# GpSimd asks for the down blocks of the first mixture, on a queue and semaphores of their own

## The reference, cut to what matters

```python
D_FF_EXPERT = 7 * D_MODEL // 2      # 3584
N_EXPERTS, TOP_K = 8, 2

def swiglu(xn, w_gu, w_down):
    g, u = jnp.split(xn @ w_gu, 2, axis=-1)
    return (jax.nn.silu(g) * u) @ w_down

def moe_swiglu(xn, router, w_gu, w_down):
    logits = (xn @ router).astype(jnp.float32)
    top_v, top_i = lax.top_k(logits, TOP_K)
    w = jax.nn.softmax(top_v, axis=-1)
    comb = jnp.sum(jax.nn.one_hot(top_i, N_EXPERTS, dtype=jnp.float32) * w[..., None],
                   axis=-2).astype(xn.dtype)
    out = jnp.zeros_like(xn)
    for e in range(N_EXPERTS):
        out = out + comb[..., e:e + 1] * swiglu(xn, w_gu[e], w_down[e])
    return out
```

## Time and profile before

| | us |
|---|---|
| median of the runs | 2438.81 (2438.15 to 2439.09, 3 runs) |
| the profiled execution | 2440.72, its span 2438.9 |
| first mixture, TensorE's first gate/up product to its last scatter | 799.9 to 1672.8 |
| HBM read over the span | 641.66 MB |
| issues of od_moe_gu into the ring and z | 196 + 28, of 1024 KB |
| issues of od_moe_down into the ring and z | 49 + 7, of 2048 KB |

### The profile page before, as it was taken

One profiled execution on the slowest core, in us unless ns is written; L12 is line 12 of the kernel. 1 busy time (PEld: TensorE's weight loads), 2 busy tenths in 40 slices (PEclk: granted clock), 3 DMA queues, 4 the chain that ended last, 5 costly groups with the idle time before them and its releaser, 6 DMA issues.

```text
span 2438.9 us, 34641 instructions
## 1 busy us (share of the span) xinstructions
PE 2341.8 (96%) x14916; PEld 1345.8 (55%) x14916; DVE 687.9 (28%) x1507; ACT 376.7 (15%) x813; POOL 1.2 (0%) x9
## 2 busy tenths in 40 slices
PE   8899999999999999999998999998989999989997
PEld 6777888888577333333333333335766336746433
DVE  2565121139765101011010101011232122273122
ACT  2101100010111111110110111111132111163211
POOL 0000000000000000000000000000000000000000
PEclk9899999999999999999999999998999999999998
DMA  9489245374366798999999999996622995832690
GB/s 319 164 296 359 72 166 214 132 265 141 115 223 250 295 380 339 374 385 408 405 409 405 408 405 409 395 395 254 235 69 75 338 317 157 214 114 75 213 357 36
DMA packets 281384, 645.13 MB, mean 265 GB/s; under 512 B 14699, under 2 KB 99969, under 8 KB 281217
## 3 DMA queue, kind: packets, MB, share of 16 engines
q1 hardware_dynamic: 278444, 637.64, 71.2%
q10 hardware_dynamic: 2773, 5.11, 0.6%
HBM read 641.66 MB, written 1.05 MB: 264 GB/s over the span
## 4 chain that ended last, share of the span: by engine, by line
PE 88%; DVE 6%; SPq 2%; ACT 2%; issue 1%; DMA 1%; ACTq 0%; DVEq 0%
PE bank L1613 20%; PE bank L1299 20%; PE bank L1715 11%; PE bank L1650 7%; PE bank L1538 6%; PE bank L1550 3%; PE bank L1319 3%; DVE att L3372 2%; PE bank L1642 2%; SPq L1205 2%; PE bank L1775 2%; PE bank L1734 1%; PE bank L1701 1%; PE bank L1861 1%; PE bank L1348 1%
## 5 line engine op out<-in xcount | busy, mean ns | idle before, releaser
L1613 PE MATMUL bank<-ring,xn 128*32 128x512 f32 (+1 forms) x3520 | 465.9, 594 | 2.3 <-DMA ring<-od_moe_gu 2.3
L1299 PE MATMUL bank<-xn,ring 128*128 128x256 f32 x2048 | 452.0, 383 | 3.3 <-ACT xn L2286 1.1
L1299 PEld LDWEIGHTS bank<-xn,ring 128*128 128x128 f32 x2048 | 392.0, 192 | 60.3 <-issue 8.1
L1613 PEld LDWEIGHTS bank<-ring,xn 128*32 128x32 f32 (+1 forms) x3520 | 140.2, 115 | 304.2 <-issue 301.5
L1715 PE MATMUL bank<-ring,att 128*32 128x512 f32 x2208 | 247.9, 593 | 1.3 <-ACT att L2416 1.3
L2979 DVE TENSOR_TENSOR sq<-att,bank 32x512 f32<-32x512 f32 x70 | 48.0, 686 | 414.4 <-ACT att L2427 412.9
L1715 PEld LDWEIGHTS bank<-ring,att 128*32 128x32 f32 x2208 | 72.3, 110 | 160.1 <-issue 159.7
L1538 PE MATMUL bank<-xn,ring 128*128 128x256 f32 x704 | 152.8, 379 | 0.0
L1538 PEld LDWEIGHTS bank<-xn,ring 128*128 128x128 f32 x704 | 134.1, 191 | 17.9
L2427 ACT ACTIVATE att<-bank 64x512 f32<-64x512 f32 (+1 forms) x123 | 72.4, 589 | 376.1 <-PE bank L1613 291.6
L2416 ACT COPY att<-bank 128x384 f32<-128x384 f32 (+1 forms) x72 | 29.9, 450 | 520.3 <-PE bank L1701 400.1
(11 more groups left out here) (352 smaller groups left out, 1968.7 us busy)
## 6 DMA issues: line engine op xcount, KB each, us to landing
ring<-od_moe_gu SPq DMA_DIRECT2D x196, 1024.0 KB, 15.5
ring<-od_moe_down SPq DMA_DIRECT2D x49, 2048.0 KB, 17.3
ring<-ada_w SPq DMA_DIRECT2D x24, 2048.0 KB, 8.2
ring<-moe_w_gate SPq DMA_DIRECT2D x32, 1024.0 KB, 11.6
ring<-moe_w_up SPq DMA_DIRECT2D x32, 1024.0 KB, 9.7
ring<-moe_w_down SPq DMA_DIRECT2D x16, 2048.0 KB, 13.8
z<-od_moe_gu SPq DMA_DIRECT2D x28, 1024.0 KB, 13.8
ring<-ev_w_in SPq DMA_DIRECT2D x10, 2048.0 KB, 20.4
```

The source lines that it names most:

```text
L1299: mm = nc.tensor.matmul(ps[:, c * T:(c + 1) * T], kblk(b)[:, k, u * T + c * P:u * T + (c + 1) * P], x[:, k, :], start=k == 0, stop=k == KD ...
L1613: mm = nc.tensor.matmul(PSB[r.fill.b][j * w:(j + 1) * w, :], xn[:, k, at:at + w], rows_[:, half, c * WBLK:(c + 1) * WBLK], start=k == 0, s ...
```

## The change

The blocks that `down_block` makes are kept in a list, `downs`. Eight new semaphores, `down_landed`, one for each slot, count the down blocks that land; `slot_landed` counts all other blocks. Each block's count (`b.landed`) is made anew from the list before the engines' programs are written. SyncE's two loops over the blocks of the first mixture leave the down blocks out. GpSimd, when its constants are set, walks through the down blocks of the same experts in the same order: it waits for the release of the earlier block of the slot, asks for the load, and adds to `down_landed`. Before the second expert it waits for `order_ready` and reads each expert's number into a register of its own, as SyncE does. TensorE's `landed` waits for the one or the other semaphore. Loads, slots, their order in the ring and all computation are as they were.

```diff
--- before.py
+++ after.py
@@ -357,6 +357,7 @@
         zero_row = no_bits.unsqueeze(1).to_broadcast([P, 4, P])
 
 
+        down_landed = [sem(f"down_landed{i}") for i in range(SLOTS + 1)]
         slot_landed = [sem(f"slot_landed{i}") for i in range(SLOTS + 1)]
         bank_full = [sem(f"bank_full{b}") for b in range(8)]
         bank_free = [sem(f"bank_free{b}") for b in range(8)]
@@ -661,8 +662,11 @@
             r.tile = [(tile_full[j], count(tile_full[j], 1) + 1) for j in range(tiles - 1)] + [(bank_full[f.b], f.n)]
             return r
 
+        downs = []
+
         def down_block(st, x, load, tiles):
             x.down = block(*load(x.c, WBLK))
+            downs.append(x.down)
             x.used = [(hid_used, st.used + x.c + 1)] + [(tile_down[j], count(tile_down[j], 1) + 1) for j in range(tiles - 1)]
             x.down.other_tiles = x.used
 
@@ -1182,6 +1186,12 @@
         rows_landed = sem("rows_landed")
 
 
+        in_slot, down_in_slot = [0] * (SLOTS + 1), [0] * (SLOTS + 1)
+        for b in blocks:
+            n = down_in_slot if b in downs else in_slot
+            n[b.slot] += len(b.loads)
+            b.landed = 16 * n[b.slot]
+
         block_ = ctx.enter_context(nc.Block())
 
         @block_.sync
@@ -1215,14 +1225,16 @@
                 free_slot(i)
                 load(i)
             for i in range(*moe1[0].blocks):
-                free_slot(i)
-                load(i, 0)
+                if blocks[i] not in downs:
+                    free_slot(i)
+                    load(i, 0)
             sp.wait_ge(order_ready, 1)
             for st in moe1[1:]:
                 expert = sp.value_load(order[0:1, st.rank:st.rank + 1], min_val=0, max_val=E1 - 1)
                 for i in range(*st.blocks):
-                    free_slot(i)
-                    load(i, expert)
+                    if blocks[i] not in downs:
+                        free_slot(i)
+                        load(i, expert)
 
             sp.wait_ge(excess_ready, 1)
             with sp.If(sp.value_load(order[0:1, E1:E1 + 1], min_val=0, max_val=T) > CAPS[0]):
@@ -1278,6 +1290,21 @@
             nc.gpsimd.tensor_copy(early_mask, con("causal")).then_inc(masks_set, 1)
             nc.gpsimd.tensor_copy(ident_bits, ident).then_inc(masks_set, 1)
 
+            def load_downs(st, expert):
+                for b in blocks[slice(*st.blocks)]:
+                    if b in downs:
+                        if b.earlier.release is not None:
+                            pool.wait_ge(*b.earlier.release)
+                        for tile in b.earlier.other_tiles:
+                            pool.wait_ge(*tile)
+                        dst, src = b.loads[0](b)(expert)
+                        pool.dma_start(dst, src).then_inc(down_landed[b.slot], 16)
+
+            load_downs(moe1[0], 0)
+            pool.wait_ge(order_ready, 1)
+            for st in moe1[1:]:
+                load_downs(st, pool.value_load(order[0:1, st.rank:st.rank + 1], min_val=0, max_val=E1 - 1))
+
         @block_.tensor
         def _(pe):
             def open_bank(f):
@@ -1287,7 +1314,7 @@
                 return PSB[f.b]
 
             def landed(b):
-                pe.wait_ge(slot_landed[b.slot], b.landed)
+                pe.wait_ge((down_landed if b in downs else slot_landed)[b.slot], b.landed)
 
             def unit(b, u, f, x, ready=None):
```

## The result

| | us |
|---|---|
| after, median of the runs | 2478.64 (2477.38 to 2480.02, 4 runs) |
| before, beside it | 2438.95 (2438.15 to 2443.07, 4 runs) |
| ratio | 1.0159, 95% interval 1.0142 to 1.0177 |
| the profiled execution after | 2477.38, its span 2475.7 |

The change makes the kernel slower by 39.7 us, and by the interval by 35 to 43. The forecast was +16, with a range up to +29: right in sign and in the place of the waits, too small by more than half.

A forecast was written before the change was run, and what follows sets the result against it. Prediction: TensorE bounds wide experts, loads the paired ones. Gains and costs of requests 0; downs passing gate/up blocks cost 10.1 + 5.8 = 15.9, say +16 us: 2454.8 us, 8 in 10 range 2436 to 2468.

The forecast's parts named there:

- What bounds the kernel: First mixture: TensorE bounds wide experts, loads bound paired ones once the ring's lead is gone; loading order can win 9.2 us.
- Part 1: SyncE no longer waits at down blocks' slots and saves 56 issues: nothing is unblocked, gain 0.
- Part 2: GpSimd makes 56 waits and requests, low end 0.37 us each; harmless under 10 us a piece: cost 0.
- Rival (c): GpSimd's requests over 10 us each or held up, downs themselves late: 2465 to 2480 us, chance 0.06.
- Part 3, no bandwidth to win: Two queues sharing the DMA engines move no more than one: 405 GB/s against 406 and 407.
- rival (b): Two requesters fill the DMA engines better, so the kernel gets faster, 2430 us at 7% more rate; chance 0.13.
- Part 3, passing downs, G17 in each paired expert: Downs on the second queue delay each paired expert's last gate/up block: +10.1 us for the first two together, +5.8 third.
- so I take equal shares while both have work: Both load queues get half the rate; last gate/up block 5.8 us late in first and third paired experts.
- one third for 2 KB rows: Upper case: queues alternate by rows, so paired experts' last two gate/up blocks get a third: +12.4 + 11 = +23.
- the transfers never pause from 1077 to 1340: Loads run unbroken through the first two paired experts, so the later date holds alone: +10.1 us, 5.8 not added.
- one common date: First two paired experts: delay set by the second's last gate/up landing, 1332.7 against 1320.4: +10.1 us together.
- The signs: Profile after: 117 MB third queue, downs landing under 12 us, gate/ups over 18, waits only at paired experts' last gate/up block.

The follow-up runs named there:

- e8: Kernel before, with the first mixture's experts reordered so that two wide ones stand between every two paired ones: 2427.69 us, ratio 0.9950.
- e11: Changed kernel with 44 products of zeros on TensorE ahead of the wait for each paired expert's last gate/up block: 2472.59 us, ratio 1.0124.

## Why the prediction was wrong

- **What bounds the kernel: held.** Of the 9.2 us of waits nothing else could be won, and e8 won them by the lead alone.
- **Part 1, SyncE's waits, 0: held.** 179 of its 224 gate/up requests now last under 0.5 us, and no time came of it.
- **Part 2, GpSimd's requests, 0: held.** 0.74 us each, twice the low end that I took, and far under the 10 us from which it would have mattered. Rival (c) is out. VectorE's port did no harm that these rows show.
- **Part 3, no bandwidth to win: held.** 401 and 402 GB/s with two queues, against 406 and 407; rival (b) is out.
- **Part 3, passing downs, G17 in each paired expert: place right, size wrong.** The step that failed is "so I take equal shares while both have work". It gave waits of 5.8 us in the first and the third paired expert; they were 11.4 and 11.1, since G16 and G17 got one third. It rested on when requests land. Had I counted the packets of that same place in the kernel before (13 to 19; ScalarE's queue is q10, SyncE's q1), I would have seen the third there:

```profile
q10 hardware_dynamic: 409, 1.62, 68.3%
q1 hardware_dynamic: 410, 0.81, 35.2%
```

- **The other value, one third for 2 KB rows, was in part lucky.** I had it as an end of the range, +23 in all. In the first paired expert it means G17 about 5 us later than 1112.0, at 1117; set on the dates of before (4.4 us added, as the mixture begins 4.4 us earlier) G17 landed at 1118.0. But two errors cancel. G13 landed at 1087.1, so G16 could begin 4 us before the 1091.5 that I took; and G16 and G17 then took 30.8 us, 15.4 a block, where I had them slowed by D18 to D20 only and not by D15 as well. And my reason was half the reason: the rows count on SyncE's queue and not on GpSimd's.
- **A second step failed: "the transfers never pause from 1077 to 1340".** The first paired expert's 15 us of delay release the slots later, and at the end of the wide expert behind it the loads have caught up, wait for slots and pause. Windows of after, and the same stretches of before:

```profile
1240.00:1290.00 50.00, 50.00 (x316) 20.29 (x310) 6.78 (x13) 5.11 (x12) 2.22 (x3) 1.00 0.96 375
1250.00:1260.00 10.00, 10.00 (x87) 5.25 (x87) 0.00 (x0) 2.48 (x7) 0.00 (x0) 1.00 0.78 299
...
1244.00:1294.00 50.00, 50.00 (x256) 18.02 (x248) 7.17 (x13) 4.74 (x9) 0.00 (x0) 1.00 1.03 409
```

Over 50 us this is 1.7 MB less, or 4.2 us of transfer, and G17 of the second paired expert landed at 1340.5 on the dates of before, 5.3 us behind the 1335.2 of the one third.

- **A term was missing: the clock behind the wait.** The rows of before had no wait long enough for it, but the paired experts' waits that I worked out, of 6 to 10 us, should have raised the question. By the rows of after it is 3.2, 2.8 and 3.2 us; e11 won back about 6.
- **The sum again.** By one third my own dates give 12.6 for the first two paired experts (1335.2 + 19.3 - 1341.9; I wrote 12.4) and 11 for the third. Measured are 20.3 and 15.3. The 20.3 are 12.6, the 5.3 of the later landing and 2.4 of slow products behind it. The first one's slow products don't count again, since the second waits for a landing anyway: in e11 the first two together are only 2.4 us shorter than after. The 15.3 are 11, 3.2 of the clock and 1.1 of small waits and rest. Together 35.6.
- **The second paired expert.** I forecast one common date for the first two and not the sum of their waits. That reasoning held: the first lost 15.0 and the second only 5.3 more. What didn't hold is that the date stays where it is.
- **The range.** It went up to +29 since I took the most that passing alone could cost as +27. The third expert's part in it, +14, is a slip: 1664.2 - 1652.3 is 11.9. The 39.7 us lie beyond the range by the clock's term, the pause, and the 4 us by which the medians differ more than the mixtures.
- **The signs.** Held: the third queue with 117 MB, no wait for a down block, the waits at G17 in the three paired experts, wide experts of 123 us. Not held: over all requests the median time to landing is 12.9 us for the downs in the ring (not under 12) and 10.4 for the gate/up blocks, less than the 15.5 of before, where I had written over 18. As I wrote it, this sign speaks against the forecast. The requests of the wide experts make it: there the ring is full, and those of 1239 to 1250 land in 7.1 to 9.3 us. Only at G16 and G17 is the landing late (17.7 to 34.5 us in the third paired expert).

## What to carry to other kernels

If one engine asks for all blocks in the order in which they are used, a second queue lets later blocks pass the one that is needed next. In this kernel, which runs close to its loads, none of the splits tried got back to the time of the one queue in order. Before splitting, find the block at which the lead is least and ask who could pass it there. Where queues must share, look at the packet size of each, for here it set the shares, and count a queue's packets in a place where two of them work; and count for each new wait on TensorE also the slow products behind it. If a stage mixes parts that gain on the loads with parts that lose, their order can be worth more than any change to the queues.

## What the runs showed of the hardware that I had not expected

- GpSimd's queue packs rows of 2 KB into packets of 4096 bytes (28672 data packets for 117.44 MB with either row length); SyncE's queue has one packet for each row of 2 or 4 KB. Two queues that both have work got packets one for one (1080 and 1077 in 16 us, and 409 and 410 in 6 us of before, with ScalarE's queue): 1 MB with 2 KB rows took 7.5 us beside a down queue, 5.5 us when its packets were 4096 bytes, 2.56 us alone.
- TensorE's granted clock was at 0.50 after it had stood still since 1102, and was back at 0.92 to 1.00 in 1120 to 1124, having worked from 1113.6 on. With 5.8 us of zeros first and 5.6 us of idle time behind them it fell too; with 9.7 us of zeros and 1.2 us of idle time it didn't. Behind 4.6 us of idle time ahead of G16 (e11, second paired expert) it was 0.50 in 1324 to 1326.
